# VectorE's order around the decay rounds, ScalarE's around the sparse scores, and where modulation units 19 to 25 are summed, in a fused two-block layer kernel

## What is computed

```python
mod = jax.nn.silu(c) @ mod_w + mod_b
shift1, scale1, gate1, shift2, scale2, gate2 = split(mod, 6)
h = rms_norm(x, g_pre_mix) * (1 + scale1) + shift1
(sc_b, sc_c, sc_x, q, k, v, z, xbc, dt_raw, gl_a, gl_b, gl_c) = split_columns(h @ w_in)
y_a = short_conv_mixer(sc_b, sc_c, sc_x, sc_conv_w) @ w_sc_out
y_b = stick_breaking_attention(q, k, v) @ w_sb_out
y_c = mamba2_mixer(z, xbc, dt_raw, ...) @ w_ssm_out
merged = sigmoid(gl_a) * y_a + sigmoid(gl_b) * y_b + sigmoid(gl_c) * y_c
x = x + gate1 * rms_norm(merged @ w_o, g_post_mix)
```

## Time and profile before

| | us |
|---|---|
| median of 3 runs | 1218.07 |
| the runs | 1217.13, 1218.07, 1776.78 |
| the profiled execution | 1217.03 |
| its span | 1215.4 |

### The profile page before, as it was taken

How to read it: one execution, slowest core, us unless ns; L and a number is a source line. 1 busy time by engine, 2 the same in 40 slices (tenths; PEclk the granted TensorE clock), 3 DMA queues, 4 the chain that set the end, 5 groups by cost and what they waited for, 6 DMA issues and landing times.

```text
span 1215.4 us, 14124 instructions
## 1 busy us (share of the span) xinstructions
PE 1072.5 (88%) x4834; PEld 715.7 (59%) x4834; DVE 875.8 (72%) x1802; ACT 517.5 (43%) x1156; POOL 339.2 (28%) x326
## 2 busy tenths in 40 slices
PE   3899979999999999998999999977968878769776
PEld 3899969878999989765565555422323323223222
DVE  5668789977888887737797758668577586685455
ACT  3338443364333345435544344433434334334344
POOL 0000100031000002203544545634434535334320
PEclk9899999999999999999999999999999998999998
DMA  9756966565888882557999999999999999999994
GB/s 380 301 194 228 366 252 242 210 250 204 313 308 321 316 318 108 212 208 289 421 410 421 423 419 421 421 421 422 421 421 422 421 421 423 420 422 421 420 422 197
DMA packets 57946, 414.10 MB, mean 341 GB/s; under 512 B 6432, under 2 KB 6432, under 8 KB 8352
## 3 DMA queue, kind: packets, MB, share of 16 engines
q0 software_dynamic: 43632, 313.02, 63.0%
q1 hardware_dynamic: 14112, 100.10, 21.9%
q10 hardware_dynamic: 144, 0.26, 0.1%
HBM read 412.30 MB, written 1.05 MB: 340 GB/s over the span
## 4 chain that ended last, share of the span: by engine, by line
PE 53%; DMA 31%; DVE 9%; ACT 5%; issue 1%; POOL 0%; SPq 0%; ACTq 0%; DVEq 0%; POOLq 0%
PE ps L1064 15%; PE ps L509 8%; PE ps L510 8%; PE ps L511 8%; DMA areas_seam<-in_experts,idx 6%; DMA gate_area<-in_experts,idx 6%; DMA spare<-in_experts,idx 6%; PE ps L495 4%; DMA ring<-in_stream 3%; DMA mod_ring<-in_experts,idx 3%; DMA ring<-in_experts,idx 3%; DMA ring<-in_experts,part_buf 2%; PE ps L765 1%; PE ps L991 1%; PE ps L619 1%
## 5 line engine op out<-in xcount | busy, mean ns | idle before, releaser
L1485 ACT ACTIVATE act<-now 128x1 f32<-128x1 f32 x256 | 50.7, 198 | 264.3 <-DVE now L2369 262.0
L1064 PE MATMUL ps<-areaB,c_row 128*128 128x512 f32 x232 | 116.1, 633 | 26.1 <-ACT c_row L1493 26.1
L1493 ACT ACTIVATE c_row<-small,act 128x128 f32<-128x128 f32 x256 | 102.8, 402 | 16.3 <-ACT act L1489 0.8
L1747 DVE CUSTOM_DVE_ANT_0 mod_ring<-mod_ring,c_row 128x1024 f32<-128x1024 f32 x84 | 99.1, 1219 | 14.6 <-DMA mod_ring<-in_mod_w 14.5
L1064 PE MATMUL ps<-ring,c_row 128*128 128x512 f32 x192 | 92.8, 614 | 14.4 <-ACT c_row L1493 13.8
L1623 POOL DMA_INDIRECT areaB<-in_experts,idx x58 | 65.3, 1126 | 124.5 <-PE ps L1064 65.8
L509 PE MATMUL ps<-hT_h,w_lo 128*128 128x256 f32 x352 | 99.1, 282 | 0.8 <-DVE hid_l L2062 0.8
L511 PE MATMUL ps<-hT_h,w_hi 128*128 128x256 f32 x352 | 98.9, 281 | 0.0
L510 PE MATMUL ps<-hT_l,w_hi 128*128 128x256 f32 x352 | 98.8, 281 | 0.0
L2369 DVE CUSTOM_DVE_ANT_0 areaB<-areaB,xn 128x1024 f32<-128x1024 f32 x58 | 70.7, 1224 | 37.3 <-DMA areaB<-in_experts,idx 37.2
L1064 PEld LDWEIGHTS ps<-areaB,c_row 128*128 128x128 f32 x232 | 43.6, 197 | 90.9 <-ACT c_row L1493 47.1
(11 more groups left out here) (436 smaller groups left out, 2591.7 us busy)
## 6 DMA issues: line engine op xcount, KB each, us to landing
ring<-in_stream SPq DMA_DIRECT2D x75, 1024.0 KB, 5.0
mod_ring<-in_mod_w POOLq DMA_DIRECT2D x40, 1024.0 KB, 5.3
gate_area<-in_mod_w SPq DMA_DIRECT2D x3, 1024.0 KB, 14.7
areaB<-in_mod_w SPq DMA_DIRECT2D x3, 1024.0 KB, 24.6
gate_area<-in_stream SPq DMA_DIRECT2D x3, 1024.0 KB, 13.0
mod_ring<-in_mod_w SPq DMA_DIRECT2D x2, 1024.0 KB, 7.6
small<-in_small SPq DMA_DIRECT2D x1, 1352.0 KB, 28.6
c_row<-in_c_rows SPq DMA_DIRECT2D x2, 512.0 KB, 17.4
```

The lines of the kernel that those rows point to most:

```text
L1064: last = mm(ps[:, B3 + 2 * b + t, :], spread_w[n // FEW % 2][:, n % FEW, :], row[ROW_OF[n]][:, D + 512 * b:D + 512 * b + 512], start=first ...
L1485: A(weight, now[n // FEW % 4][:, here], ACT.Gelu).then_inc(gelu_done, 1)
L1493: A(spread_w[n // FEW % 2][:, n % FEW, :], c_("ident"), ACT.Identity, scale=weight)\
L1747: V.tensor_tensor_reduce(w, w, silu, 1.0, 0.0, ALU.mult, ALU.add, column).then_inc(mod_summed, 1)
```

## The change

On ScalarE, the two z blocks are copied out as they are, and one Silu over both follows; before, each copy was a Silu. The copy of z0 now stands ahead of the Ln, and the split of gl1 ahead of the copy of z1.

```diff
             step(A(sbl, sbl, ACT.Exp, scale=-1.0))
             split_front(AT["gl", 0])
-            step.wait()
-            A(sbl, sbl, ACT.Ln, bias=1.0).then_inc(sb_log, 1)
             for j in range(2):
-                copy_out("z", j, zg[:, 2 * j:2 * j + 2, :], func=ACT.Silu, bank=n % 2)
+                if j == 1:
+                    split_front(n + 2)
+                copy_out("z", j, zg[:, 2 * j:2 * j + 2, :], bank=n % 2)
                 if j == 0:
-                    split_front(n + 3)
+                    act.wait_ge(act_step, step.n)
+                    A(sbl, sbl, ACT.Ln, bias=1.0).then_inc(sb_log, 1)
                 n += 1
+            act.wait_ge(evac, n)
+            step(A(zg, zg, ACT.Silu))
```

```diff
+            front_lo("gl", 7)
             mod_unit(18)
-            front_lo("gl", 7)
+            front_lo("gl", 8)
...
-            front_lo("gl", 8)
-            mod_units(19, 21)
             dve.wait_ge(bc_mm, 1)
             for h in range(8):
-                if h == 4:
-                    front_lo("gl", 9)
                 if h % 4 == 0:
                     dve.wait_ge(dec_exp, h // 4 + 1)
...
-            mod_unit(21)
+            front_lo("gl", 9)
+            mod_unit(19)
             front_lo("gl", 10)
-            mod_unit(22)
             dve.wait_ge(y_mm, 1)
...
             front_lo("gl", 11)
-            mod_unit(23)
             dve.wait_ge(ysum_mm, 1)
...
             split_br(0)
-            mod_units(24, 26)
+            mod_units(20, 23)
             split_br(1)
...
             for j in range(4):
                 if j in (1, 2):
                     split_br(j + 1)
+                if j == 1:
+                    mod_unit(23)
+                if j == 2:
+                    mod_unit(24)
                 if j == 3:
+                    mod_unit(25)
                     split_wo(0)
```

## The result

| | us |
|---|---|
| the kernel before, median of 5 runs | 1217.13 |
| the changed kernel, median of 5 runs | 1225.16 |
| ratio, with its 95% interval | 1.0074 [1.0063, 1.0086] |
| profiled execution of the changed kernel | 1225.16 |
| its span (before: 1215.4) | 1223.4 |

The changed kernel is slower by 0.7%: inside the 2% that were called no change, but a real difference by its interval. It is 3.4 us above the forecast of 1221.8 and inside the range. The span grew by 8.0 us and the medians lie 8.03 apart, so the profiled execution can stand for the whole. One of the five runs of before (1776.78) is a disturbed one and is left out of the ratio.

A forecast was written before the change was run, and what follows sets the result against it. VectorE, without slack, was taken to bound the stage, ending it together with TensorE. 2.5 (wo1's low part) + 1.5 (clock) + 0.8 (feed-forward load) = +4.8 on 1217.03 gave 1221.8 us, range 1215.5 to 1227.

The forecast's parts named there:

- rival 3: The loads collide: unit 22 lands after 9.1, VectorE waits 7.6, wo0 is slow throughout; +8.9 us, 1225.9; chance 0.18.
- ScalarE: gl0's 1.03 us wait for z0's copy goes, TensorE waits 0.3 to 0.4 at gl2: -0.6 us, bounds 0 to 1.03.
- gl8's low part out of VectorE's line: Moved ahead of the decay arguments into VectorE's 3.48 us wait for TensorE's L720: -2.27 us of VectorE's line.
- wait for the B-C products: Decay weights now follow their arguments at once but need TensorE's B-C products: a new VectorE wait, +1.3 us.
- wait for unit 22's load: Ahead of the second branch split VectorE waits for this late modulation load: +4.1 us, bounds 3.5 to 7.6.
- wo1's low part: VectorE's first low part of the second output block comes +2.5 us later, bounds +1.9 to +6.0.
- clock in wo0: After TensorE's 5.1 us idle wait, wo0 runs partly at half speed: +1.5 us, between 0 and 2.9.
- first feed-forward load: At wo1's end a 1 MB modulation load may be in front of it: +0.8 us, between nothing and 4.1.
- Carried to the end unchanged: Behind this stage everything follows by waits of the same order, so the +4.8 us reaches the end unchanged.
- Rivals 1: TensorE, not VectorE, sets the stage's end, so its stall goes for good: 1208.7 us; chance 0.05.
- 2: Unit 22 does not hold VectorE, because its load lands by 199: -1.6 us, 1215.5; chance 0.12.
- 4: The order does nothing to the end, since unseen slack takes up both signs: 1217 to 1218 us; chance 0.05.

The follow-up runs named there:

- the unit-20 run: Changed kernel with modulation unit 20 summed behind gl11's low part instead of behind the first branch split: 1219.74 us, ratio 1.0013 to the kernel before.
- the dummy-product run: Changed kernel with ten dummy products (20 matmuls in the trace) in TensorE's pause ahead of wo0: 1220.51 us, ratio 1.0031 to the kernel before.
- the unit-26 run: Changed kernel with modulation unit 26 moved behind wo3's low part: 1222.85 us, ratio 1.0042 to the kernel before.
- both moves: Changed kernel with unit 20 behind gl11's low part and unit 26 behind wo3's low part: 1216.87 us, ratio 1.0002 to the kernel before.
- the last run: Changed kernel with units 20, 25 and 26 moved and dummy products ahead of wo0: 1215.01 us, ratio 0.9986 to the kernel before.

## Why the prediction was right, and by how much it was off

The mechanism was right: VectorE has no slack in this stage, so the long wait that went from TensorE's middle could not shorten it, and the change lost time by a new wait. The size was less good. The sum was 4.8 and 8.0 was measured; 1225.16 lies just above the 1218.5 to 1225 that got 0.60, and nearer to rival 3's 1225.9 than to the forecast. That nearness is chance: rival 3 has +6.0 by unit 22 and +2.9 by the clock, and measured were 3.43, 1.53 and 3.02 of a load that it does not have. The terms one by one, predicted and measured:

| step | predicted | measured | seen in |
|---|---|---|---|
| ScalarE | -0.6 | -0.47 at the decay arguments | VectorE's rows; not resolved by e1's interval |
| gl8's low part out of VectorE's line | -2.27 | -2.27, but another wait took it | VectorE's rows |
| wait for the B-C products | +1.3 | +1.27 | VectorE's rows |
| wait for unit 22's load | +4.1 (3.5 to 7.6) | +4.70 | VectorE's rows; 5.4 in total by the unit-20 run |
| wo1's low part | +2.5 | +3.43 | VectorE's rows |
| clock in wo0 | +1.5 (0 to 2.9) | +1.53 | chain; the dummy-product run |
| first feed-forward load | +0.8 (0 to 4.1) | +3.02 | chain; the unit-26 run |
| sum | +4.8 | +8.0 | |

- **ScalarE.** (e1 is the run of ScalarE's order alone.) gl0's wait for z0's copy is gone as predicted. But where 0.3 to 0.4 was expected ahead of gl2, TensorE waits 1.3 for gl0's copy (the last row of its waits above): the wait moved rather than went. Nor is the 0.47 the work of ScalarE's order: ScalarE's Exp of the sparse scores, ahead of every edited line, began 1.80 earlier in this execution than in that of before (98.23 against 100.03), and most of this lead went into the 1.3. In e1, which was 0.06 ahead at the Abs (97.21 against 97.27), no such wait stands and 0.95 is left at the decay arguments. Nothing of the term is seen in the total.
- **gl8's low part.** The prediction put it into the 3.48 us of waiting for L720, and of these 3.08 are still there. What took it is a wait further ahead, which the prediction did not look at: before, VectorE waited 2.47 for unit 18's load. Now gl7's low part stands ahead of that unit and fills the wait, and gl8's stands where gl7's was. The term would have held by the wait for L720 too, so its value is right and its place is not. The rows of before, then of the changed kernel (the low parts are L1824 and L1827, the unit L1747 and L1750):

```profile
152.06 1.23 DVE L1747 CUSTOM_DVE_ANT_0 mod_ring<-mod_ring,c_row 128x1024 f32<-128x1024 f32 x1 [2.47 <-DMA mod_ring<-in_mod_w]
...
154.36 2.35 DVE L1824 TENSOR_TENSOR ring_lo<-ring,front_hi 128x1024 fp32r<-128x1024 f32 x2
```

```profile
149.44 2.35 DVE L1827 TENSOR_TENSOR ring_lo<-ring,front_hi 128x1024 fp32r<-128x1024 f32 x2
151.70 1.22 DVE L1750 CUSTOM_DVE_ANT_0 mod_ring<-mod_ring,c_row 128x1024 f32<-128x1024 f32 x1
...
154.29 2.36 DVE L1827 TENSOR_TENSOR ring_lo<-ring,front_hi 128x1024 fp32r<-128x1024 f32 x2 [0.22 <-ACT front_hi L1216]
```

- **The decay rounds.** The wait at the decay weights is 0 (under 1 predicted), that at the y sums 1.76 (1.4 predicted).
- **Unit 22.** Its load was issued at 197.65 and held the chain for 6.23 us, a little under the median of 6.5 in the earlier trace rows. The term was mis-sized by 0.6, because I stayed near the lower end. By the estimate of 4.4 for the load the wait would have been 2.9 (196.6 + 0.8 + 4.4 - 198.9), 1.2 below the term and not 0.6 as the prediction has it.
- **The waits in the gate branch.** 1.79 ahead of br1's third product and 2.58 ahead of br2, where some 3 and 2 were predicted ahead of br2 and br3. None stands ahead of br3: the mean clock was 0.59 from 213.6 to 217.0, in br2, and the first eight products of br2 took 3.57 us where those of br1 took 1.90. That br2 ran longer by it is the likely reason, and was not tried. The wait ahead of wo0 is 4.98 (5.1 predicted).
- **The clock in wo0.** +1.53 against +1.5 is luck in part. I took the middle between nothing and 2.9, and the 2.9 has the clock falling 4.1 us into the wait, with 5.8 us of wo0 slow. It fell 2.3 into it, and 4.2 us of wo0 were slow: from wo0's start to wo1's it took 8.56 instead of 6.60, and 1.53 of these 1.96 reached wo1's end. In the execution with both moves the same item came to 2.27.
- **What failed: "most likely part of it: +0.8".** This is the mis-sized term, 2.2 of the 3.2 us that the sum lacked. The text saw that the modulation load would come in front if wo1 is late and unit 26 is not, and then took a fifth of the bound instead of asking who is issued first. The new order decided it: unit 26 follows VectorE's splits (its end moved by 3.4, with VectorE), wo1 follows those and the clock (its end moved by 5.0). The issue for unit 28 lay 0.52 behind wo1's end before, so 1.5 of slow clock was enough to pass it. From the forecast's own numbers that could be worked out.
- **Rival 3** put the collision at unit 22's load. That load was issued 1.8 behind the third branch block's (195.9, which took 4.8) and took 6.23, 1.2 above the least in the earlier trace rows; the dear collision happened at the end of the stage. Rivals 1, 2 and 4 need an end of the stage that comes earlier or less than 2 later, and it came 8 later.
- **Carried to the end unchanged**: right, 7.98 at ScalarE's first feed-forward operand and 8.0 at the end of the span. That they agree to 0.02 is chance: from this operand to the end it took 968.5 in the kernel before and 968.6 in the changed one, but 966.8 to 971.1 in the executions of the other runs, without the one that was held up behind it.

## What to carry to other kernels

A stall that goes on one engine is worth nothing when another engine is busy through the whole stage: ask which engine's work gets shorter, and where the work that was moved away still has to stand. When two loads are issued within a microsecond, work out which comes first, and for each small delay of the chain whether it reverses them; this was worth 3 us here, twice the 1.5 of slow clock that caused it. Before a step is moved later, read the lists of the other engines for what stands behind the waits that it releases; two units put 30 us later cost 15.6 us of TensorE through GpSimd's list.

## What the runs showed of the hardware

- Two 1 MB loads on different queues, the feed-forward load of SyncE and a modulation load of GpSimd, were issued close together in many of the runs. Issued first, the feed-forward load kept its time: 4.88, 4.85 and 4.69 with the other 0.52, 0.55 and 0.54 behind (the kernel before, ScalarE's order alone, the dummy products), and the other took 8.0, 8.0 and 6.7. Issued second, it took 8.34, 8.11, 7.90, 7.42 and 7.18 with the other 0.53, 0.63, 1.00, 1.57 and 1.75 ahead. The other then took 5.0 to 5.2, but 7.2 in the closest case. So it was mostly the second that paid. Issued 2.8 behind, in the last run, it took 4.8, as if alone; why 1.75 costs 2.4 and 2.8 nothing is open.
- The Trainium skill (DMA: Bandwidth & Descriptors, Queues, rings and completion order) says that each DMA engine takes turns between the queues with work, packet by packet; by that both loads should be slowed. The trace agrees only in the closest case with GpSimd's load first (7.2 and 8.34); in the others the first one kept its time.
- The clock fell 2.3 us into the idle 5 us ahead of wo0 and was down for 6.8 us (230.1 to 236.9); twenty dummy products in that pause (4.48 us in a row) kept it at 1.00.
